# A hybrid decoder step on one core: state stores issued by SyncE, sixteen state visits in twelve beats, gate units ahead of the attention branch's units

## What is computed

```python
u = hn @ w_in
z_ssd, xbc, dt_raw, q, k, v, z_att, g_ssd, g_att = jnp.split(u, _split_points(), axis=-1)
...
y, new_ssm = _ssd_chunked(xh, dt, A, B, C, ssm_state)      # new_ssm: prompt and samples
br_ssd = (y.astype(x.dtype) @ w_ssd_br).astype(F32)
br_att = (o.astype(x.dtype) @ w_att_br).astype(F32)
mix = jax.nn.sigmoid(g_ssd) * br_ssd + jax.nn.sigmoid(g_att) * br_att
out = x + mix.astype(x.dtype) @ w_out
```

## Time and profile before

| | us |
|---|---|
| median of 3 runs | 1098.62 (1093.25 to 1102.05) |
| the profiled execution, device time | 1096.22 |
| its span, first to last instruction | 1094.4 |
| PE busy | 1010.6 (92% of the span) |
| DVE busy | 701.6 (64%) |
| ACT busy | 532.5 (49%) |
| POOL busy | 246.8 (23%) |
| mean granted clock of PE | 0.984 of full |

### The profile page before, as it was taken

The page is one execution under the profiler, slowest core; times in us unless marked ns, Lnnn a source line. Parts: engine busy times, 40 slices in busy tenths (PEclk is TensorE's granted clock), DMA queues, the critical chain, the costliest instruction groups (busy, mean ns, idle before and its releaser), DMA issues.

```text
span 1094.4 us, 21697 instructions
## 1 busy us (share of the span) xinstructions
PE 1010.6 (92%) x8444; PEld 939.3 (86%) x8444; DVE 701.6 (64%) x1117; ACT 532.5 (49%) x1271; POOL 246.8 (23%) x327
## 2 busy tenths in 40 slices
PE   3999988898989899999999999999999998599998
PEld 2999888888989887469998998998999998599998
DVE  6857476564656559577887787887855566823432
ACT  5335555464645655125556456456445667412110
POOL 0222122222223101002202202202201988300000
PEclk9999999999999999999999999999999999799999
DMA  9542335236341037672472472472387997432221
GB/s 377 231 184 116 121 148 221 81 131 256 130 180 54 26 129 252 219 274 86 176 281 92 160 292 80 165 286 111 146 343 307 338 369 294 153 119 77 84 101 49
DMA packets 30261, 198.00 MB, mean 181 GB/s; under 512 B 4520, under 2 KB 6792, under 8 KB 20688
## 3 DMA queue, kind: packets, MB, share of 16 engines
q1 hardware_dynamic: 25664, 183.09, 44.1%
q0 software_dynamic: 4496, 13.54, 3.2%
HBM read 179.89 MB, written 104.70 MB: 260 GB/s over the span
## 4 chain that ended last, share of the span: by engine, by line
PE 60%; DVE 16%; ACT 14%; issue 7%; DMA 3%; SPq 0%; POOL 0%; DVEq 0%; ACTq 0%; POOLq 0%
PE bank L682 32%; PE bank L716 8%; PE bank L729 5%; ACT wH L1262 4%; DVE cacc L1677 4%; ACT Sx L1426 2%; DMA slot<-in_state_ssm 1%; DVE yL L2108 1%; PE bank L1000 1%; PE bank L982 1%; PE bank L905 1%; PE bank L805 1%; PE bank L974 1%; PE bank L845 1%; DVE Sx L1809 1%
## 5 line engine op out<-in xcount | busy, mean ns | idle before, releaser
L1656 DVE TENSOR_TENSOR wL<-w_raw,wH 128x2048 fp32r<-128x2048 f32 (+1 forms) x63 | 144.3, 2291 | 108.1 <-ACT wH L1262 106.1
L682 PE MATMUL bank<-xH,wH 128*128 128x260 f32 x976 | 203.6, 290 | 4.0 <-DVEq L1601 1.4
L682 PE MATMUL bank<-xH,wL 128*128 128x260 f32 x976 | 196.3, 283 | 0.0
L682 PE MATMUL bank<-xL,wH 128*128 128x260 f32 x976 | 195.8, 282 | 0.0
L1262 ACT CAST wH<-w_raw 128x2048 fp32r<-128x2048 f32 (+1 forms) x63 | 119.0, 1889 | 90.5 <-PE bank L682 82.4
L682 PEld LDWEIGHTS bank<-xH,wH 128*128 128x128 f32 x976 | 150.0, 188 | 13.6 <-issue 11.3
L716 PE MATMUL bank<-wH,xH 128*128 128x256 f32 x480 | 144.5, 301 | 18.0 <-DVEq L1601 11.0
L682 PEld LDWEIGHTS bank<-xL,wH 128*128 128x128 f32 x976 | 150.3, 188 | 0.0
L682 PEld LDWEIGHTS bank<-xH,wL 128*128 128x128 f32 x976 | 150.1, 188 | 0.0
L716 PE MATMUL bank<-wL,xH 128*128 128x256 f32 x480 | 138.9, 289 | 0.0
L716 PE MATMUL bank<-wH,xL 128*128 128x256 f32 x480 | 138.6, 289 | 0.0
(11 more groups left out here) (296 smaller groups left out, 2056.7 us busy)
## 6 DMA issues: line engine op xcount, KB each, us to landing
w_raw<-in_weights SPq DMA_DIRECT2D x62, 1024.0 KB, 5.1
out_kvs<-in_cache SPq DMA_DIRECT2D x16, 2044.0 KB, 10.5
ring<-in_cache SPq DMA_DIRECT2D x48, 256.0 KB, 4.0
slot<-in_state_ssm SPq DMA_DIRECT2D x16, 512.0 KB, 6.2
out_ssm_s<-slot POOLq DMA_DIRECT2D x16, 512.0 KB, 6.3
out_kvs<-in_cache SPq DMA_DIRECT2D x8, 508.0 KB, 7.0
out_kvp<-st POOLq DMA_DIRECT2D x18, 128.0 KB, 3.8
out_kvp<-vv POOLq DMA_DIRECT2D x18, 128.0 KB, 5.3
```

The costliest lines, as they stand in the source:

```text
L682: mm = pe.matmul(bk[hf].tile[:, 0:HALF], wslot(w, i)[:, k, s * P:(s + 1) * P], x[:, k, hf * HALF:(hf + 1) * HALF], start=(k == 0 and n == ...
L1656: TT(wL[:, i % 2, 0:k * n], raw[:, i % 2, 0:k * n], wH[:, i % 2, 0:k * n].bitcast(F32), ALU.subtract)\
```

## The change

Four things change in the plan, and one on POOL and SP.

1. The attention branch's two items come after all four `ga` items: the beats are now gs 2 unit 1, gs 3 (2 units), ga 0 to 3 (8 units), ba 0 and 1 (8 units). The splits follow: ga 0, ga 1, ga 2, ga 3, ba 0, ba 1, bs 0, bs 1.
2. The 16 visits are spread over the first 12 beats (one, one, two, and so on), no longer one a beat over 16.
3. The store of a state is issued by SP (`sstore`), two beats after its read and just ahead of the next `sload`; POOL no longer issues it. POOL gets a wait for its previous addition before the next outer product, in place of the one that stood before the store.
4. The parts are spread two a beat over the eight `ba` beats.

```diff
     items += [("gs", j) for j in range(4)]
-    for j in range(2):
-        items += [("ga", 2 * j), ("ga", 2 * j + 1), ("ba", j)]
+    items += [("ga", j) for j in range(4)] + [("ba", j) for j in range(2)]
...
+VISIT_BEATS = 12
...
-    for j in range(2):
-        rest += [("ga", 2 * j + half, unit) for half in range(2) for unit in range(2)]
-        rest += [("ba", j, unit) for unit in range(4)]
+    rest += [("ga", j, unit) for j in range(4) for unit in range(2)]
+    first_ba = len(rest)
+    rest += [("ba", j, unit) for j in range(2) for unit in range(4)]
+    visits = [range(UNITS * b // VISIT_BEATS, UNITS * (b + 1) // VISIT_BEATS) if 0 <= b < VISIT_BEATS else range(0) for b in range(len(rest))]
     for beat, (kind, j, unit) in enumerate(rest):
         use = proj(kind, j, unit=unit)
-        if beat < UNITS:
-            if beat and beat % PER_GROUP == 0:
-                out.append(("sgroup", beat // PER_GROUP))
-            out.append(("sread", beat))
-        if beat % PER_GROUP == 1 and beat < UNITS:
-            out.append(("sbcopy", beat // PER_GROUP))
-        if 0 < beat <= UNITS:
-            out.append(("sdecay", beat - 1))
-        if SLOTS_S <= beat - 2 < UNITS:
-            out.append(("sload", beat - 2))
-        if kind == "ba" and j == 1 and unit > 0:
-            out.append(("sfinal", unit - 1))
+        for u in visits[beat]:
+            if u and u % PER_GROUP == 0:
+                out.append(("sgroup", u // PER_GROUP))
+            out.append(("sread", u))
+        for u in visits[beat - 1] if beat else ():
+            if u % PER_GROUP == 0:
+                out.append(("sbcopy", u // PER_GROUP))
+            out.append(("sdecay", u))
+        for u in visits[beat - 2] if beat > 1 else ():
+            out.append(("sstore", u))
+            if SLOTS_S <= u + SLOTS_S - 1 < UNITS:
+                out.append(("sload", u + SLOTS_S - 1))
+        if 0 <= beat - VISIT_BEATS < 3:
+            out.append(("sfinal", beat - VISIT_BEATS))
         out.append(use)
-        left = len(rest) - 1 - beat
-        if left <= 4:
-            out += [("parts", u) for u in range(4 * (4 - left), 4 * (5 - left)) if u < UNITS]
-    out += [("sload", UNITS - 1)] if len(rest) - 2 < UNITS else []
+        if beat >= first_ba:
+            out += [("parts", 2 * (beat - first_ba) + e) for e in range(2)]
...
+                elif op == "sstore":
+                    u = a[0]
+                    sp.wait_ge(S["sample_state_ready"], u + 1)
+                    sp.dma_start(ssms_out[u], slots[u % SLOTS_S][:, :, :]).then_inc(S[f"state_kept{u % SLOTS_S}"], 16)
...
                     if u == 0:
                         pool.wait_ge(S["sample_xdt_ready"], 1)
+                    else:
+                        pool.wait_ge(S["sample_state_ready"], u)
...
-                    pool.wait_ge(S["sample_state_ready"], u + 1)
-                    pool.dma_start(ssms_out[u], st_u[:, :, :]).then_inc(S[f"state_kept{u % SLOTS_S}"], 16)
```

## The result

The changed kernel takes 1110.09 us in the median of 4 runs (1107.25 to 1110.72), beside 1097.88 us for the kernel before on the same chip: a ratio of 1.0113, with a 95% interval of 1.0085 to 1.0141. It is 12.2 us slower; forecast were 12.1.

A forecast was written before the change was run, and what follows sets the result against it. A loop of load, cast, decay, addition, store and next load was to bind: last read at 934.4, plus 27.0 + 1.8 + 0.4 + 1, puts `bs` 0 at 964.6, 12.1 us later; 1098.62 + 12.1 gives 1111, range 1095 to 1126.

The forecast's parts named there:

- load of ga 1 on SP: Issue of this split's load, behind the addition and store of state 0: 848.9, 18.3 us later than before.
- interval to ga 2: From ga 1's load to ga 2's: load 5.1, cast, decay, two additions, outer product and issues, 17.9 us.
- to ga 3: From ga 2's load to ga 3's: 14.8 us by computing, taken as 16 for a store behind a cache copy.
- to ba 0: From ga 3's load to ba 0's: 16.1 us by computing, 18.3 by transfers, taken as 18.
- to ba 1: From ba 0's load to ba 1's: work as in the first interval, load 7.0 to landing, 19.8 us.
- load of ba 1 to the last read: Load 7.0, cast 1.90, subtraction 2.3 and DVE's last two reads 2.58: 13.8 us, last read at 934.4.
- last read to `bs` 0: DVE's 27.0 us of work, 1.8 waiting for bs 0's weights, 0.4, and 1 for PE's lower clock.
- the end of DVE: DVE's work behind the last read: 27.0 us against 20.9 before, including sixteen low parts at 0.62, 10.0 us.
- the state store's wait behind a copy: On SP's queue, stores wait for cache copies landing 13.2 us after issue; intervals to ga 3 and ba 0 became 16 and 18.
- A: Rival: loads land early, PE's pace holds; last read about 911, bs 0 at 938, 14 us less, 1084; chance 0.14.
- C: Rival: POOL sets the visits' pace; last read about 920, bs 0 at 947, time 1093; chance 0.26 together with B.
- B: Rival: the loop binds but transfers are short, so no change, 1094 to 1104; chance 0.26 together with C.

The follow-up runs named there:

- e1: Changed kernel with each split's load issued one split earlier on SP, from ga 0 on; 1099.88 us, 1.0010 of the kernel before.
- e3: Kernel before with only the stores moved to SP, each followed by a state load; 1112.34 us, ratio 1.0123.
- e4: Changed kernel with six pieces of the cache copy moved behind the loads of bs 1 to bs 6; 1108.13 us, ratio 1.0091.
- e12: e9 with the first two low parts one beat later on DVE, behind the sums of the state output; 1088.06 us, ratio 0.9908.
- e2: Changed kernel with the stores issued by POOL again, order of the beats as changed; 1107.88 us, ratio 1.0091.
- e7: e5 with the stores issued by POOL again; 1100.68 us, ratio 1.0037 to the kernel before.
- e5: Changed kernel with the edits of e1 and e4 together: split loads earlier, copies later; 1093.78 us, ratio 0.9975.
- e11: Changed kernel, loads as they were, with samples' parts early and eight odd low parts on POOL; 1107.95 us, ratio 1.0100.
- e8: e5 with the 16 visits spread over 16 beats again; 1102.69 us, ratio 1.0036 to the kernel before.
- e9: e5 with the samples' parts at the fourth beat from the last visit, not behind the last ba unit; 1089.56 us, ratio 0.9931.

## Why the prediction was right

**Right in mechanism and in sum.** Forecast and measured, step by step:

| step | predicted | measured |
|---|---|---|
| load of ga 1 on SP | 848.9 | 846.74 (848.8 in the time of before) |
| interval to ga 2 | 17.9 | 18.5 |
| to ga 3 | 16 | 15.8 |
| to ba 0 | 18 | 18.4 |
| to ba 1 | 19.8 | 18.3 |
| load of ba 1 to the last read | 13.8 | 13.9 |
| last read to `bs` 0 | 30.2 | 31.9 |
| `bs` 0 to the end | unchanged | +0.05 us |
| `bs` 0 against before | +12.1 | +13.1 from the mark |

The first load, three of the four intervals and the way to the last read came within a microsecond, and the fourth, 1.5 us shorter, offset the end, which was 1.7 longer. Some of that closeness is luck. In the interval to ga 2 the load took 6.28 us for my 5.1, while two additions and an outer product took 6.75 for my 7.42, since the means of the earlier trace rows hold operations that were stretched. In the last interval the same three took 6.73, and the load 6.03 for my 7.0: that is the 1.5 us. PE's gaps came at the spread (6.91 us, forecast 5) and ahead of the third `ba` unit (13.25 us, forecast over 10), with a clock of 0.75 of full speed in the mean of that stretch, that is, part of it at the lower of its two levels. Experiment e1 shows that the loads' place is the cause, e3 that the store's issue alone is enough, and e4 that the copies are a small part.

**Right by the wrong working: the end of DVE.** I had 27.0 us of work at 0.62 us a low part, 1.8 us of waiting for the weights of `bs` 0, and 1 us for the clock. The wait did not come (DVE lost 0.52 us for PE there), and the first pair of low parts and the operation behind it took far longer. DVE in the changed kernel, and POOL beside it:

```profile
935.56 3.37 DVE L2113 TENSOR_TENSOR yL<-ygn,yH 128x512 fp32r<-128x512 f32 x2
938.85 2.45 DVE L2097 TENSOR_TENSOR y<-y,dsb 128x128 f32<-128x128 f32 x1
```

```profile
936.22 2.16 POOL L1249 TENSOR_TENSOR outer<-Bsp,XD 128x1024 f32<-128x1024 f32 x1
938.46 2.69 POOL L1254 TENSOR_TENSOR slot<-slot,outer 128x1024 f32<-128x1024 f32 x1
```

3.37 against 1.29 and 2.45 against 0.28: 4.25 us more, beside POOL's last outer product and addition. That is the term I left out; e12 shows that such times come from POOL. The trace of the kernel before already had it, in a line between those I read:

```profile
935.45 5.75 DVE L2108 TENSOR_TENSOR yL<-ygn,yH 128x512 fp32r<-128x512 f32 x4
```

These four took 3.25 us more than four with POOL idle (2.50). So the term belongs in the 31.9 us of the changed kernel, but of the growth from 21.0 to 31.9 it is only 1.0 us; most of the rest is the added work that I had counted (four uses, four low parts and a subtraction, 9.3 us).

**The order of stores and copies.** I put the state store's wait behind a copy into two intervals. In that to ba 0 it is there (9.94 us in the chain at 889.17), and its size was about right: without copies the interval fell by 1.6 us. In that to ga 3 it is not what the chain lies on: store 4 landed 11.7 us after its issue at 868.93, but just as SP had issued store 5 (880.20), and the chain goes by a load of 8.13 us (my 7.0) and computing. The 16 us were right there, their reason only in part; without copies it fell by 0.8. The median store, however, landed 3.8 us after its issue, sooner than POOL's 6.3; the wait behind a copy is a matter of single stores. The page I weighed says that another issuer saves only the issue time (the Trainium skill, DMA: Bandwidth & Descriptors, "Issuing engines are not separate DMA queues"). For the time of the kernel that holds roughly: e2 puts the issuer back and gains 2 us at most. For the landing the rows differ from it: in the same order of work the median store from POOL landed 7.5 us after its issue (e2), from SP 3.8, and without copies 4.6 (e7) against 3.0 (e5). Of the program it says nothing, and there the cost was: what is queued behind the issue and its wait.

**The rivals.** A, the pace of PE, did not occur in the changed kernel, and not in e5 either: POOL sets the pace there. C, POOL's pace, which I had counted into B, is what remains with loads and copies out of the way (e5, e7); it was forecast at 1093, and e5 measured 1093.78, but partly by luck: in the time of before its last read is at 915.4 (920 forecast) and `bs` 0 at 950.0 (947), 34.6 us after the read where I had 27.4. B's lower bound, loads with nothing in the way, is nearest to e4; its intervals were 17.7, 15.0, 16.8 and 19.3 us, not the 17.9, 12.9, 14.2 and 17.9 I gave, since the median load still took 7.2 us there. The time of e4 is 2 us less, not 14.

**Still open.** The gain of e11 over the changed kernel (2 us in the medians, none in the trace's `bs` 0) is within the intervals. How much of e8's loss is POOL's operations beside DVE's low parts, which lie in every beat there, and how much the banks, was not separated. And e7's 6.3 us were not split: its state loads also wait for stores that land later (4.6 us in the median against 3.0 in e5).

## What to carry to other kernels

Before an issue with a wait is moved to another engine's queue, list what stands behind it there: if a load behind it feeds the work that it waits for, the two close a loop, and its length, walked from rows, is the new pace. Saved issue time counts only on the engine that sets the pace; here it was seen to pay only with the loads drawn ahead of the stores and the copies moved (e5 against e7). And a duration taken from a row holds for what ran beside it there: four low parts took 2.50, 5.75 or 9.0 us, according to what POOL did.

## What the runs showed of the hardware

- **POOL holds up some of DVE's operations, and the reverse.** With both inputs in SBUF (`yL<-ygn,yH`, `y<-y,dsb`) an operation of DVE ended only just after a running one of POOL: 2.0 to 2.4 us for 0.29 (e12), 5.11 for a pair that takes 1.29 (e9). Those with an input in a PSUM bank (`sc<-slot,bank` 1.28, `mix<-mix,bank` 0.42) and the reduction (1.22) kept their times beside POOL. When DVE's subtraction of a split (2.29 us, 908.87 in e12) was first, POOL's outer product took 3.83 us instead of 1.90. The Trainium skill, SBUF — State Buffer, "Who interferes with whom", says that an instruction of DVE with two inputs in SBUF contends with one of GpSimd that reads SBUF, as an exclusive lock; the rows agree. It should have been in my sum: 4.25 of the 31.9 us behind the last read.
- **The landing of a store depends on what was issued just ahead.** The same 512 KB from SP landed 3.0 us after issue in the median in e5, 3.8 in the changed kernel, 7.5 in e1, and single ones after 14.5, where a split's load and a copy stood right ahead of them. Between e1 and e5 only the copies moved.
- **PE's clock after a gap.** PE in the changed kernel, behind its wait of 13.25 us, and 5 us after the end of its next wait (943.32):

```profile
936.19 0.64 PE L683 MATMUL bank<-oL,wH 128*128 128x260 f32 x2
936.62 0.64 PE L683 MATMUL bank<-oH,wL 128*128 128x260 f32 x2
...
948.85 0.40 PE L683 MATMUL bank<-oH,wH 128*128 128x260 f32 x2
949.09 0.40 PE L683 MATMUL bank<-oL,wH 128*128 128x260 f32 x2
```

A pair starts every 0.43 us in the first place and every 0.24 in the second; the granted clock was 0.50 there (936.2 to 940.9) and 1.00 here (948.6 to 949.8), the two levels, 1.2 and 2.4 GHz. It did not come back once for all: from 944.4 to 945.1 it was 1.00, and from 945.2 to 948.2, with PE busy throughout, 0.50 again. e11 gives the granted clock from such a gap to `bs` 0: 0.78 in the mean.
